# A hybrid attention and retrieval block: value rows mixed into the first rows, a shorter ring of value units

## The reference

```
qr = (hb @ w_pq) ...                 # 8 heads, two halves
sc = einsum(qr, sub_keys)            # scores of 128 sub-keys in each half
s_top, i_top = top_k(sc, 16)         # the 16 best of each half,
c_top, c_pos = top_k(sums, 16)       # and of their 256 sums the 16 best
expert = i0 * 128 + i1               # one of 16384 experts
g = softmax(c_top)
u = u_tab[expert]                    # rows of 2048 floats
a = gelu(einsum('bthkd,btd->bthk', u, hb))
out = einsum('bthk,bthkd->btd', g * a, v_tab[expert])
```

## Time and profile before

| | us |
|---|---|
| median of three runs (1504.0 to 1505.83) | 1504.36 |
| the profiled execution | 1503.99 |
| its span, first to last instruction | 1502.2 |
| TensorE busy | 1436.2 |
| VectorE busy | 1163.3 |
| ScalarE busy | 495.5 |
| GpSimd busy | 438.6 |

### The profile page before, as it was taken

How to read it: one execution, slowest core, us unless ns; L and a number is a source line. 1 busy time by engine, 2 the same in 40 slices (tenths; PEclk the granted TensorE clock), 3 DMA queues, 4 the chain that set the end, 5 groups by cost and what they waited for, 6 DMA issues and landing times.

```text
span 1502.2 us, 21800 instructions
## 1 busy us (share of the span) xinstructions
PE 1436.2 (96%) x8017; PEld 1104.3 (74%) x8017; DVE 1163.3 (77%) x1825; ACT 495.5 (33%) x1434; POOL 438.6 (29%) x431
## 2 busy tenths in 40 slices
PE   9999999999999999999999999989888999999997
PEld 7789888888899999999999999974333344444443
DVE  5735588576687899999387777759666889898988
ACT  6857566764654200000144454438000000000000
POOL 2000100000001222323211111146544666666662
PEclk9999999999999999999999999999999999999999
DMA  9735744648769989999999999999999999999996
GB/s 361 261 105 139 194 130 140 210 135 323 258 205 356 357 360 421 421 421 422 422 421 420 421 420 421 420 409 415 418 417 414 406 391 395 396 407 375 397 398 260
DMA packets 115545, 513.14 MB, mean 342 GB/s; under 512 B 26524, under 2 KB 28700, under 8 KB 63724
## 3 DMA queue, kind: packets, MB, share of 16 engines
q0 software_dynamic: 58640, 297.85, 49.6%
q1 hardware_dynamic: 47456, 150.94, 28.0%
q10 hardware_dynamic: 9360, 63.20, 10.2%
HBM read 628.91 MB, written 3.41 MB: 421 GB/s over the span
## 4 chain that ended last, share of the span: by engine, by line
PE 51%; DMA 38%; DVE 6%; issue 2%; ACT 1%; POOL 1%; SPq 0%; DVEq 0%; POOLq 0%; ACTq 0%
PE ps L1672 15%; DMA late<-in_v_tab,acts 12%; DMA late<-in_u_tab 10%; PE ps L1710 9%; DMA raw<-in_u_tab 6%; PE ps L1453 5%; PE ps L1448 5%; PE ps L1450 5%; DMA raw<-in_v_tab,acts 3%; DMA acts<-in_v_tab,acts 3%; DVE ps L1269 3%; PE ps L1618 2%; PE ps L1614 2%; PE ps L1613 2%; DMA raw<-in_w_in 1%
## 5 line engine op out<-in xcount | busy, mean ns | idle before, releaser
L931 DVE TENSOR_TENSOR w_lo<-raw,w_hi 128x512 fp32r<-128x512 f32 (+1 forms) x288 | 186.9, 681 | 114.3 <-ACT w_hi L609 113.0
L1672 PE MATMUL ps<-acts,late 128*128 128x128 f32 x1952 | 227.5, 276 | 9.7 <-DMA late<-in_u_tab 7.9
L1672 PEld LDWEIGHTS ps<-acts,late 128*128 128x128 f32 x1952 | 221.6, 192 | 14.3 <-ACT acts L836 6.2
L1672 PE MATMUL ps<-acts,raw 128*128 128x128 f32 x1920 | 223.7, 276 | 7.1 <-DMA raw<-in_u_tab 6.1
L1672 PEld LDWEIGHTS ps<-acts,raw 128*128 128x128 f32 x1920 | 217.8, 192 | 11.5 <-ACT early L836 4.0
L609 ACT ACTIVATE w_hi<-raw 128x512 fp32r<-128x512 f32 (+1 forms) x288 | 169.1, 621 | 84.4 <-PE ps L1618 33.5
L1710 PE MATMUL ps<-raw,acts 128*128 128x512 f32 x352 | 160.9, 610 | 18.2 <-DMA raw<-in_v_tab,acts 18.2
L1269 DVE SCALAR_TENSOR_TENSOR ps<-acts,sel,ps 128x2048 f32<-128x2048 f32 x63 | 148.3, 2355 | 19.9 <-DMA acts<-in_v_tab,acts 15.5
L1710 PE MATMUL ps<-late,acts 128*128 128x512 f32 x336 | 151.6, 601 | 11.6 <-DMA late<-in_v_tab,acts 11.6
L1269 DVE SCALAR_TENSOR_TENSOR ps<-late,sel,ps 128x2048 f32<-128x2048 f32 x63 | 148.4, 2355 | 16.5 <-DMA late<-in_v_tab,acts 12.2
L1710 PE MATMUL ps<-acts 128*128 128x512 f32 x336 | 148.3, 593 | 0.8 <-DMA acts<-in_v_tab,acts 0.7
(11 more groups left out here) (239 smaller groups left out, 2013.8 us busy)
## 6 DMA issues: line engine op xcount, KB each, us to landing
raw<-in_w_in SPq DMA_DIRECT2D x72, 512.0 KB, 4.5
raw<-in_u_tab SPq DMA_DIRECT2D x31, 1024.0 KB, 11.6
late<-in_u_tab SPq DMA_DIRECT2D x31, 1024.0 KB, 11.4
late<-in_u_tab ACTq DMA_DIRECT2D x30, 1024.0 KB, 11.6
raw<-in_u_tab ACTq DMA_DIRECT2D x29, 1024.0 KB, 11.8
raw<-in_w_o SPq DMA_DIRECT2D x32, 512.0 KB, 4.8
raw<-in_w_pq SPq DMA_DIRECT2D x32, 512.0 KB, 5.2
acts<-in_u_tab SPq DMA_DIRECT2D x7, 1024.0 KB, 8.3
```

What stands on the lines that cost most here:

```text
L931: V.tensor_tensor(wlo[slot_no][:, 0:w], raw[j % NRAW][:, half * w:half * w + w], whi[slot_no][:, 0:w].bitcast(F32), ALU.subtract).then_inc ...
L1672: ins = mm(ps[:, q, 0:N_DN], unit[:, k * P:k * P + P], hF[:, k, :], start=k == 0, stop=k == KD - 1)
```

## The change

Three things change together.

1. `ROWS`: behind the first 84 u rows (0 to 83) a u row and a value row alternate, until the 128 u rows are through (rows 84 to 171); then come the 84 value rows that are left. The number of rows, their gathers and the pace of 1.33 rows for each unit stay.
2. `held` is the sum of the value rows throughout the second pass. All u rows therefore read the scaled token from SBUF (`hs`); ScalarE's copy into PSUM and the waits for it go.
3. `V_RING` is 5, since `hs` stays in use: the ring has no sixth buffer. Unit `u` waits for TensorE to be through with unit `u - 5`.

```
-    V_RING = 6
+    V_RING = 5
...
-        ring += [region(A_HF, 2 * UNIT), hs]
+        ring += [region(A_HF, 2 * UNIT)]
...
-        U_FIRST = N_PICK
+        ROWS_SB = 83
+        U_FIRST = ROWS_SB + 1
         ROWS = [("u", n) for n in range(U_FIRST)]
         for n in range(U_FIRST, N_PICK):
             ROWS += [("u", n), ("v", n - U_FIRST)]
...
-                elif u == NRING + 1:
-                    pool.wait_ge(hs_moved, 4)
-                    pool.wait_ge(row_used, ROWS_SB)
                 else:
                     pool.wait_ge(unit_used, NKEY + u + 1 - V_RING)
...
-            act.wait_ge(gelu_done, NKEY)
-            for n in range(4):
-                nc.scalar.activation(ps[:, n, :], hs[:, 512 * n:512 * n + 512], ACT.Copy).then_inc(hs_moved, 1)
...
-                        V.scalar_tensor_tensor(row[BUF[r]], row[BUF[r]], 1.0, held if moved else hs, ALU.mult, ALU.mult,
+                        V.scalar_tensor_tensor(row[BUF[r]], row[BUF[r]], 1.0, hs, ALU.mult, ALU.mult,
                                                accum_out=a_sel[:, n:n + 1]).then_inc(row_used, 1)
...
-            dve.wait_ge(hs_moved, 4)
-            next_row(8, True)
+            dve.wait_ge(gelu_done, NKEY)
+            next_row(8)
             list_units(2)
-            next_row(14, True)
+            next_row(14)
```

More of the change, by code:

```diff
@@ L288, in build_block @@
         hF_done, rs_mm, rs_row_done, hF_raw, gain_row_in, hs_ready, idx_ready = sem("hF_done"), sem("rs_mm"), sem("rs_row_done"), sem("hF_raw"), sem("gain_row_in"), sem("hs_ready"), sem("idx_ready")
-        hs_moved = sem("hs_moved")
         warm_set, gsp_ready, a_done, value_ready = sem("warm_set"), sem("gsp_ready"), sem("a_done"), sem("value_ready")
@@ L385, in build_block @@
         V_ROW = [ROWS.index(("v", n)) for n in (0, N_PICK - 1)]
-        ROWS_SB = 83
         WEIGH_AT = {0: 100, 1: 100, 2: 125}
@@ L1252, in _, with next_row @@
             rows_done = [0]
-            def next_row(count=1, moved=False):
+            def next_row(count=1):
                 for r in range(rows_done[0], rows_done[0] + count):
@@ L1404, in _ @@
             weigh(2)
-            dve.wait_ge(hs_moved, 4)
-            next_row(8, True)
+            dve.wait_ge(gelu_done, NKEY)
+            next_row(8)
             list_units(2)
-            next_row(14, True)
+            next_row(14)
             list_units(3)
             for h in range(3, NH):
-                next_row(U_LAST[h] + 1 - rows_done[0] + (5 if h < NH - 1 else 0), True)
+                next_row(U_LAST[h] + 1 - rows_done[0] + (5 if h < NH - 1 else 0))
                 weigh(h)
```

## The result

| | before | after |
|---|---|---|
| median, five runs each | 1505.15 us (1504.0 to 1506.35) | 1512.75 us (1510.72 to 1513.82) |
| the profiled execution | 1503.99 | 1513.82 |
| its span | 1502.2 | 1512.0 |

The ratio is 1.0053, with a 95% interval of [1.0042, 1.0064]: 8.0 us slower.

A forecast was written before the change was run, and what follows sets the result against it. DMA was taken to bound the u part; in the value part all were near their limit. Mixed part +5.6, ring +3.2 and turn 0 gave +8.8 us, 1513 against the median; range 1501 to 1524.

The forecast's parts named there:

- the hold as summed: Whole kernel: u operations with two SBUF inputs delay gathers as the sum counts, 1508 to 1520 us; chance 0.50.
- four rivals: Mixing gains, 1500 (0.13); nothing changes, 1505 (0.20); five unit buffers too few, 1523 (0.10); held gathers cost more, 1524 (0.07).
- the signs that the prediction had named: Mixed part: gathers of 1.5 to 2.9 us, GpSimd over 70% busy, 4.08 us a unit; value part: landings near 12 us.
- The ring, +3.2: Value part: five buffers require landing within 12.3 us; +0.05 us for each of 63 units, +3.2 us (0 to +45).
- The mixed part, -4.1 and +9.7, net +5.6: Rows 84 to 171, 65 units: 4.08 us each instead of 3.99, +5.6 us (-4.1 to +28).
- DMA in the mixed part: Mixed rows: spreading the bytes gives 3.93 us a unit by DMA alone, -4.1 us over 65 units.
- GpSimd in the mixed part: Mixed rows: u operations hold back gathers and fill GpSimd, so a unit takes 4.08 us instead of DMA's 3.93.
- the counts of 3.92 and 3.97: Mixed rows: GpSimd's time for a unit with held gathers, taken at random 3.92 us, as a cycle of rows 3.97.
- The turn, 0: Change of passes: VectorE gets sums some 2 us sooner, sixth unit goes out later, near 1018 us; 0 (-2 to +2).
- VectorE and the end, 0: Row operations keep 2.29 and 2.36 us, about 3.2 us a unit, hidden by data waits; last rows unchanged; 0.
- value rows hold nothing back: Second pass: value row operations read PSUM as well, so they delay no gather.

The follow-up runs named there:

- the ring alone: The kernel before with five unit buffers instead of six, token still in PSUM, u rows first: ratio 1.0022, +3.3 us.
- mixed kernel with six buffers: Kernel before with u and value rows alternating from row 84, six unit buffers, token in PSUM, value rows not summed: 1.0017, +2.6 us.
- mixed kernel with five buffers and no hold: Changed kernel with the token in PSUM, so no gather is held by u rows, and value rows not summed: 1.0023, +3.5 us.
- the hold without the mixing: Changed kernel with all u rows first again, token in SBUF, five unit buffers: 1.0100, +15.0 us against the kernel before.
- moved to the other operation: Kernel before, mixed from row 104, six unit buffers, token in PSUM, value rows summed in SBUF while both kinds alternate: 0.9996, -0.6 us.
- the two divided holds: Changed kernel, value rows not summed, token in SBUF only from row 104 (1.0027, +4.1 us) or only up to row 103 (1.0047, +7.1 us).
- all holds: Changed kernel with the sum over value rows left out, token in SBUF throughout: 1.0062, +9.3 us against the kernel before.

## Why the prediction was right in its number, and where not in its parts

*The forecast.* 1513 was said, 1512.75 came. By its time, the chance named "the hold as summed" is what happened, and of the four rivals none did: landings shortened to 12 us, so the ring did not decide; the gathers were held; and 1512.75 is near none of their times (1500, 1505, 1523, 1524). But the sum met the time because two of its parts erred in opposite ways, -4.1 and +9.7 where the runs show about 0 and 5.9. That they cancel is luck. All the signs that the prediction had named came too (held gathers, GpSimd busy for 152.6 of 190 us, 4.08 us for a unit, landings near 12 us), and none of them told that the cost arises at the turn.

*The ring, +3.2.* Right in size: +3.3 alone. The landing time fell from 15.9 us to between 11.6 and 12.5, where 12.3 was needed. The step put it into the value part; there the changed kernel's unit pace went from 3.527 to 3.579 us (gathers of units 65 and 127 at 1263.40 and 1485.28 us, before 1253.24 and 1471.94), as said. With the ring alone it was 3.539, and most of the loss came earlier. The mixed kernel with six buffers had 3.606, so the 3.579 does not speak for the ring. The term has its size alone; its place isn't shown. In the mixed order the sixth buffer was worth 0.9 us, the difference of 1.0023 and 1.0017, which is within their intervals.

*The mixed part, -4.1 and +9.7, net +5.6.* The net is right: the changed kernel stands 4.7 to 7.4 us over the ring alone. Its unit pace was 4.084 us (unit 8 at 1030.63, 65 at 1263.40), where 4.08 was predicted, and the baseline of the same units was 3.966 and not 3.99. But the mixed kernel with five buffers and no hold had 4.033 there (1025.92 to 1255.82), and the ring alone 4.032: in this stretch the hold adds some 0.05 us to a unit, not 0.15, and that 4.08 came is luck too. (The last unit is issued 13.3 us later than before, and the span grew by only 9.8, since gathers land 3 to 4 us sooner.) Both halves of the net failed:

- "DMA in the mixed part": -4.1 us, as if bytes could be spread without loss. The runs show +0.2 with five buffers and +2.6 with six. The gain is there between 1070 and 1260 us (413 against 408 GB/s), and it is given back at the turn, where by the reading above lighter rows leave the DMA engines short, and in the value part. That the value part has no more to give, since TensorE needs 3.44 of its 3.53 us, stood in the prediction's first two paragraphs; the step did not use it.
- "GpSimd in the mixed part": +0.15 us for each of 65 units over the DMA's 3.93, 9.7 in all, evenly. The mechanism is shown four times (the hold without the mixing, with it, divided, and moved to the other operation), but it cost 5.9 us, and some 3.6 of them within the first 70 us. Behind the turn GpSimd was saturated, as the counts of 3.92 and 3.97 said. That did not matter, because DMA was full at the same pace: a gather landed 10.7 to 12.1 us after its issue, so one that is issued 2 us late still found the engines busy. Landing from 1060 to 1160 us:

```profile
late<-in_v_tab,acts POOLq DMA_INDIRECT x18, 10.9
...
late<-in_u_rows,sel POOLq DMA_INDIRECT x9, 12.1
```

*The turn, 0.* This is the step that failed most. The wait of VectorE for the sums went from 6.67 to 5.21 us, though it ended 1.2 us later than before, not sooner, and the sixth unit went out at 1018.05, as said. But the step counted edits and left out the hold, which is densest just there: VectorE works through its landed rows back to back there, one pair in 4.67 us, and first waits for data at 1055.65 us:

```profile
1016.87 0.18 DVE L1278 TENSOR_SCALAR acts<-acts 128x17 f32<-128x17 f32 x1 [5.21 <-ACT early L872]
...
1055.65 2.29 DVE L1253 SCALAR_TENSOR_TENSOR acts<-acts 128x2048 f32<-128x2048 f32 x1 [2.69 <-DMA acts<-in_u_rows,sel]
```

Fifteen of 38 gathers were held while the queue in front of the DMA engines was still to be filled; without holds at the turn it is 2 of 42. The step also set the lighter value rows among the first gathers against the heavier u rows later, while the runs with six buffers suggest that they cost 2.6 us. The answer to the earlier trace rows is the first of these rows.

*VectorE and the end, 0.* Nothing speaks against it: the row operations took 2.290 and 2.355 us, and in the changed kernel too the last ones follow one another without a pause.

The page "SBUF — State Buffer" of the Trainium skill, section "Who interferes with whom", infers that generating descriptors needs only the write side and so would go on beside such an operation. The runs here contradict it for the indirect gathers: whichever operation had two SBUF inputs held them, and with one of these in PSUM none was held (in the kernel before, 231 gathers from 1000 to 1470 us start during such an operation). The very first value row of the changed kernel, which reads its start value from SBUF, held one too (2.16 us at 1023.42), and so did that of the kernel before (1.43 us at 1159.86), so that "value rows hold nothing back" was true of all but one. The same section says that the order of issue decides which of the two blocks the other. Here blocking is seen in one direction only: the row operation that starts 0.16 us into a gather (1055.65 us) takes its usual 2.29.

**What stays open.** Whether the 1.7 us between the two divided holds and all holds are real. Whether the changed kernel's +8.0 and +10.7 us differ by more than noise (their intervals meet). That lighter rows starve the DMA engines at the turn is supported by the rates there, but no run changed the bytes alone. Where the ring alone loses, which rests on one profile; in the mixed order its price could not be told from nothing. And a sixth buffer beside the token in SBUF that adds no wait at the turn was not tried.

## What to carry to other kernels

A hidden cost is hidden only where a queue is deep enough to cover it: price it where the queue is being built up, at the change of phase, and not by the mean of the phase. Bytes that are moved from a part bound by transfers to another bring only what that other part has left, and a lighter transfer in a fixed number of buffers may starve the engines. A sum that meets the time does not prove its terms: here each had to be measured by a kernel that changes it alone. When both operands of a long VectorE operation come to lie in SBUF, look at what GpSimd issues beside it.

## What the runs showed of the hardware

- A gather that GpSimd starts while a VectorE operation with two SBUF inputs (2.28 to 2.35 us) runs ends 0.81 to 0.88 us behind it (48 gathers of the changed kernel, from 1000 to 1470 us): it takes up to 3.12 us instead of 0.95 to 0.99. It is the same for the multiply with accumulated output and for the scaled add.
- The inputs decide, not the output: value rows with one input in PSUM that write into SBUF hold no gather (mixed, no hold, ring of five: none of 109 from 1070 to 1260 us).
- It is the start of the gather that decides. In the changed kernel one started at 1055.49 us, 0.16 before the operation of 1055.65, and took 0.99 us beside it. The operation is not slowed either: of 23 with two SBUF inputs that start 0.11 us or more into a gather there, none takes over 2.29 us.

```profile
1055.49 0.99 POOL L554 DMA_INDIRECT late<-in_v_tab,acts  x1 [0.30 <-issue]
```

- From 1070 to 1260 us the DMA engines stayed at a share of 1.01 and 407 GB/s with 30 of 109 gathers held. From 1000 to 1070 us they had 0.95 and 363 GB/s with 15 of 38 held, and 0.99 and 396 in the same order and ring with 2 of 42.
